# Weight pieces behind the experts' read-back, and Pool's scatter ahead of its gather

## The reference

```python
def _moe(h, router_w, router_bias, w_gate, w_up, w_down):
    x = h.reshape(b * n, d)
    scores = jax.nn.sigmoid(x @ router_w)
    ...  # best group of experts, then the two best experts in it
    gates = jnp.sum(jax.nn.one_hot(idx, N_EXPERTS) * wsel[..., None], axis=1)
    a = jnp.einsum('td,edf->tef', x, w_gate)
    up = jnp.einsum('td,edf->tef', x, w_up)
    mid = jax.nn.silu(a) * up * gates[:, :, None]
    y = jnp.einsum('tef,efd->td', mid, w_down)

def layer(x, l, mod, mixer):
    y, aux = mixer(_rmsnorm(x, norm_mix[l]) * (1.0 + sc1) + sh1)
    x = x + g1 * y
    h = _rmsnorm(x, norm_ffn[l]) * (1.0 + sc2) + sh2
    x = x + g2 * _moe(h, ...)
```

## Time and profile before

| | us |
|---|---|
| median of three runs | 930.47 |
| the three runs | 928.52, 930.5, 930.47 |
| the profiled execution | 928.82 |
| its span, first to last instruction | 927.0 |

### The profile page before, as it was taken

The page is one execution under the profiler, slowest core; times in us unless marked ns, Lnnn a source line. Parts: engine busy times, 40 slices in busy tenths (PEclk is TensorE's granted clock), DMA queues, the critical chain, the costliest instruction groups (busy, mean ns, idle before and its releaser), DMA issues.

```text
span 927.0 us, 11593 instructions
## 1 busy us (share of the span) xinstructions
PE 803.5 (87%) x4091; PEld 447.8 (48%) x4091; DVE 379.2 (41%) x848; ACT 272.2 (29%) x636; POOL 108.1 (12%) x157
## 2 busy tenths in 40 slices
PE   4779999999888996999988599888899978999860
PEld 0236665544443464555536346545554555555430
DVE  3366583265064243332212644664651432322114
ACT  1241212121451042222211536565540332222111
POOL 2300000001000003101013002212200022010120
PEclk9989999999978997899999799999989998999995
DMA  9991222259991347899997966202109388999975
GB/s 275 370 341 50 71 93 95 90 172 345 258 371 53 130 134 250 315 405 410 411 387 262 347 246 246 93 1 93 48 1 346 125 288 312 396 411 410 384 257 208
DMA packets 84561, 220.19 MB, mean 238 GB/s; under 512 B 9636, under 2 KB 19549, under 8 KB 84185
## 3 DMA queue, kind: packets, MB, share of 16 engines
q1 hardware_dynamic: 73570, 197.04, 58.9%
q0 software_dynamic: 9120, 18.75, 5.9%
q10 hardware_dynamic: 1816, 3.68, 1.1%
HBM read 214.77 MB, written 14.89 MB: 248 GB/s over the span
## 4 chain that ended last, share of the span: by engine, by line
PE 63%; DMA 15%; DVE 8%; ACT 4%; SPq 3%; issue 3%; DVEq 1%; POOLq 1%; POOL 0%; ACTq 0%
PE ps L923 57%; PE ps L930 4%; DMA arena<-in_moe_w_up_dram 3%; DMA ring<-in_w_mod_dram 2%; DMA h_rows<-xn 2%; PE ps L1150 2%; DMA ring<-in_moe_w_down_dram 2%; DMA xn<-y_rows 2%; SPq L643 1%; DVEq L1909 1%; DVE negmax L1962 1%; SPq L660 1%; DMA hT<-h_rows,rows_in 1%; SPq L690 1%; ACT hT L1626 1%
## 5 line engine op out<-in xcount | busy, mean ns | idle before, releaser
L923 PE MATMUL ps<-arena 128*64 128x256 f32 (+12 forms) x1164 | 237.6, 449 | 24.8 <-ACT hT L1626 5.9
L923 PEld LDWEIGHTS ps<-arena 128*64 128x64 f32 (+4 forms) x1164 | 128.6, 168 | 115.9 <-issue 71.9
L923 PE MATMUL ps<-ring,hT 128*128 128x512 f32 (+2 forms) x384 | 133.6, 507 | 4.5 <-issue 3.9
L923 PE MATMUL ps<-ring,arena 128*64 128x256 f32 (+1 forms) x784 | 111.3, 431 | 5.5 <-DMA ring<-in_moe_w_down_dram 4.2
L923 PEld LDWEIGHTS ps<-ring,hT 128*128 128x128 f32 x384 | 73.0, 192 | 62.9 <-issue 58.5
L923 PEld LDWEIGHTS ps<-ring,arena 128*64 128x64 f32 x784 | 53.9, 137 | 51.3 <-issue 28.3
L930 PE MATMUL ps<-ident,arena 128*128 128x128 f32 (+2 forms) x332 | 51.0, 293 | 17.2 <-DVE hT L1968 4.6
L1582 ACT ACTIVATE arena<-ps 128x256 f32<-128x256 f32 (+4 forms) x88 | 38.5, 454 | 85.9 <-PE ps L923 82.2
L923 PE MATMUL ps<-hT,ring 128*128 128x384 f32 x192 | 62.1, 486 | 0.0
L2294 DVE TENSOR_TENSOR arena<-arena,ps 128x128 f32<-128x128 f32 x37 | 10.6, 288 | 124.1 <-ACT arena L1688 124.1
L923 PE MATMUL ps<-ring,condT 128*32 128x512 f32 x384 | 52.7, 674 | 8.6 <-DMA ring<-in_w_mod_dram 7.9
(11 more groups left out here) (301 smaller groups left out, 871.7 us busy)
## 6 DMA issues: line engine op xcount, KB each, us to landing
ring<-in_w_mod_dram SPq DMA_DIRECT2D x48, 1024.0 KB, 9.4
ring<-in_moe_w_down_dram SPq DMA_DIRECT2D x22, 1024.0 KB, 16.8
ring<-in_moe_w_gate_dram SPq DMA_DIRECT2D x38, 512.0 KB, 12.9
ring<-in_moe_w_up_dram SPq DMA_DIRECT2D x38, 512.0 KB, 15.5
arena<-in_moe_w_gate_dram SPq DMA_DIRECT2D x36, 512.0 KB, 9.5
arena<-in_moe_w_up_dram SPq DMA_DIRECT2D x36, 512.0 KB, 10.9
arena<-in_moe_w_down_dram SPq DMA_DIRECT2D x15, 1024.0 KB, 13.7
ring<-in_ev_w_in_dram SPq DMA_DIRECT2D x9, 1024.0 KB, 13.3
```

The costliest lines, as they stand in the source:

```text
L923: mm = pe.matmul(out, lhsT, rhs, **kw)
```

## The change

Two places. On SP, `rows_back(0, nb)` is called ahead of the pieces in1.0 and in1.1 instead of behind them. In Pool's overflow loop the pair of waits and the scatter of block b come first, and the pair of waits and the gather of block b + 1 behind it. The waits stay with their DMA.

```diff
@@ SP
                 if i == at["after0"]:
                     nb = send_over(0)
+                if i == at["in1.0"]:
+                    rows_back(0, nb)
                 if i == at["in1.1"] + 1:
-                    rows_back(0, nb)
                     for t in range(NT):
                         sp.wait_ge(y_back[t], 32)
@@ Pool
                 with pool.Fori(1, nb) as b:
                     pool.drain()
+                    pool.wait_ge(over_done[l], b + 1)
+                    pool.wait_ge(y_read[1][l], b + (NE + 1))
+                    pool.tensor_tensor(pool_mark[:, 0:1], pool_mark[:, 0:1], pool_mark[:, 0:1], ALU.mult)
+                    pool.indirect_dma_start(y_rows, bass.IndirectOffsetOnAxis(ap=to_now[0:HALF, :], axis=0), ysb[0:HALF, 0, :], None,
+                                            bounds_check=2 * T - 1, oob_is_err=False).then_inc(over_stored[l], 16)
                     pool.wait_ge(row_ready[l], b + 2)
                     pool.wait_ge(xt_full[1][l], b + (NPAIR + 2))
-                    pool.tensor_tensor(pool_mark[:, 0:1], pool_mark[:, 0:1], pool_mark[:, 0:1], ALU.mult)
+                    pool.tensor_tensor(pool_mark[:, 1:2], pool_mark[:, 1:2], pool_mark[:, 1:2], ALU.mult)
                     pool.indirect_dma_start(xg_over, None, h_rows[l], bass.IndirectOffsetOnAxis(ap=row_now[:, :], axis=0), bounds_check=T - 1, oob_is_err=False).then_inc(
                         over_gathered[l], 16)
-                    pool.wait_ge(over_done[l], b + 1)
-                    pool.wait_ge(y_read[1][l], b + (NE + 1))
-                    pool.tensor_tensor(pool_mark[:, 1:2], pool_mark[:, 1:2], pool_mark[:, 1:2], ALU.mult)
-                    pool.indirect_dma_start(y_rows, bass.IndirectOffsetOnAxis(ap=to_now[0:HALF, :], axis=0), ysb[0:HALF, 0, :], None,
-                                            bounds_check=2 * T - 1, oob_is_err=False).then_inc(over_stored[l], 16)
```

## The result

The changed kernel takes 940.35 us (median of six runs, 938.91 to 946.6), the kernel before beside it 930.49 us. The ratio is 1.0139, with a 95% interval from 1.0103 to 1.0175: 10 to 16 us slower. The forecast was 934.9 us with a range up to 937.4: the direction was right, the size less than half.

A forecast was written before the change was run, and what follows sets the result against it. Bound by hand-overs between Pool, TensorE and the DMA queues at the ends of both layers' experts. Layer 0 +0.45 and layer 1 +3.95 make +4.4 us, set on the 930.47 us median: 934.9 us, range 931.0 to 937.4.

The forecast's parts named there:

- part 2: Pool's overflow loop, scatter first, then gather: +1.05 us in layer 0, +2.9 and +1.05 us in layer 1.
- ACT's reads start 1.05 us late, SP's don't: Layer 0's read-back: ACT waits for the loop's last gather; +1.05 us charged whole, bounds 0 and 1.6; same in layer 1.
- the ring: Sign in layer 0: the latent projection should show no wait on it; waiting for the in1 pieces would refute the forecast.
- My bound of zero: ACT's late read-back in layer 0: lowest cost 0, since SP's head start uses the same bandwidth and nothing is lost.
- The gather of block 1 sooner: Layer 0: without 1.7 MB of in1 pieces beside it, the gather lands 0.6 us sooner; bounds 0 and 1.54.
- The scatter without the gather ahead of it: Layer 0's last scatter: losing the gather ahead is worth nothing, 498.25 at the earliest against 498.35.
- The in1 pieces hidden: Layer 0: the moved pieces land at 517.6, before the latent projection at 521.48; 3 to 4 us of slack, no cost.
- Rival 3: Layer 0: in1 pieces at half rate land at 522, TensorE stands some 2 us; 936.9 us, chance 0.10.
- The late gather of block 2: Layer 1: starts at 896.32 instead of 891.96, lands in 4.05 us; down product +2.9 us, bounds +1.0 and +3.7.
- Rival 1: Both layers: the late gathers are hidden, layer 0 -0.6 and layer 1 +1.0 us; 930.9 us, chance 0.16.
- Rival 2: Layer 0's traffic is the bound: 1.54 us from the in1 pieces, 1.8 from Pool's loads; 927.2 us, chance 0.08.

The follow-up runs named there:

- e5: The kernel before with only ACT's three reads held back by four tiny activations (0.48 us) in both layers; 935.48 us, ratio 1.0053.
- e6: The kernel before with SP's three reads held until ACT has issued its own; 936.11 us, ratio 1.0067.
- e3: The changed kernel with ACT's wait for the gathers moved behind its three reads in both layers; 932.53 us, ratio 1.0028 against the kernel before.
- e11: The kernel before with the in1 pieces behind the read-back and Pool's nine MLA loads held until the read-back has landed; 929.86 us, ratio 1.0017.
- e2: The kernel before with only the in1 pieces moved behind the read-back, the loop still gather first; 928.94 us, ratio 0.9993.
- e1: The kernel before with only the loop order changed to scatter first, the in1 pieces still ahead of the read-back; 939.68 us, ratio 1.0114.
- e8: The kernel before with Pool's nine small MLA loads held until the read-back has landed; 929.78 us, ratio 0.9974.
- e10: The changed kernel with ACT's wait for the gathers behind its reads in layer 0 only; 936.65 us, +6.3 us against the kernel before.
- e7: The changed kernel with 52 instead of 28 filling products on TensorE in layer 0's read-back; 942.96 us, ratio 1.0120 against the kernel before.

## Why the prediction was wrong

**The step that failed** is in part 2: "ACT's reads start 1.05 us late, SP's don't ... so I charge all of it", and the same for layer 1. The place was right, and the delay nearly so: 0.95 us in both layers. The price was wrong. I charged the length of the delay, and held 0 and 1.6 us for its bounds. It costs 2.6 us in layer 1, and in layer 0 4.25 us at the latent products, of which about 1 us goes with the in1 pieces. The signs that the prediction named for this all came: ACT's reads 1 us behind SP's, a wait for the gather of block 2, none for the ring. None of them was the landing of ACT's first tile.

The forecast assumed that from the moment ACT's reads are issued, each queue gets half. The traces show that with a head start of 0.95 us SP's first two tiles go out alone. In layer 1 SP's tiles landed about 3.7, 5.0 and 7.5 us after its start, ACT's first at 7.65; before, with both together, SP's landed at 4.7, 7.3 and 9.8, ACT's first at 5.1. e5 gives the slope with nothing else changed, e6 shows it with the roles changed, and e3 takes it away.

The bytes weren't lost: in layer 1 the last of the six tiles is there 10.1 us after the start in both kernels. The order changed, and each join needs both halves of the first tile. My bound of zero ("SP's head start uses the same bandwidth and nothing is lost") reasoned from the total, where the chain hangs on the first tile.

The Trainium skill ("DMA: Bandwidth & Descriptors", Queues, rings and completion order) says that a DMA engine takes turns between its queues, packet by packet. I let that rule stand for an even division from ACT's start on. The traces agree with the turns once both queues move: 5 to 6 us after the start (920.24 to 921.24) SP's moved 0.20 MB and ACT's 0.22. They don't show them from ACT's issue on. This is what the queues moved in the first 4 us (packets, MB, share of 16 engines; q1 is SP's, q10 ACT's), in the kernel before from 905.61 to 909.61:

```profile
q1 hardware_dynamic: 126, 0.50, 46.9%
q10 hardware_dynamic: 107, 0.44, 28.0%
```

and in the changed one from 915.24 to 919.24, where q10 has no row, though ACT had issued its first tile after 0.95 us:

```profile
q1 hardware_dynamic: 252, 0.97, 73.2%
```

ACT's queue began when SP's had moved about 1.1 MB, two tiles. In e5, issued 0.52 us late, it began after 0.6 MB, about one tile, and in e6 SP's began after 1.3 MB of ACT's. That fits tiles that go out in the order of their issue, whichever queue they are on. No run tests this by itself, and why the later queue starts so late isn't settled.

**What I left out** is TensorE's clock. I had not weighed this row: the latent products of the kernel before take 7.22 us for 16, though those behind them need 11.41 us for 32. In the profiled execution the changed kernel pays 1.24 us and 1.7 us in layer 0, and 1.1 us on the last down product in layer 1 (3.02 us instead of 1.94). The first two come back later. Nor do they follow from the delay alone: in e6 TensorE stood 11.68 us ahead of the transposes and these products took 7.27 and 5.76 us, nearly as before; in e11 it stood 6.26 us, less than before, and they took 8.77 and 7.46. The third goes with the long wait for the late gather (see e3).

**Point by point.**
- *The gather of block 1 sooner.* Forecast -0.6 us. It took 7.43 us instead of 7.84 and TensorE waited 1.04 us instead of 1.54: 0.4 to 0.5 us, right. It didn't help the total: e2 is -0.7 us with 2.4 us to each side.
- *The scatter without the gather ahead of it.* Forecast worth nothing. VectorE ended 0.11 us sooner and the scatter started 0.11 us sooner: right, with the 0.53 us between mark and issue that an idle Pool needs.
- *The in1 pieces hidden.* No wait on them is in any trace, right as far as TensorE is concerned. Rival 3 looked at TensorE, which doesn't wait for them. What they cost is seen at ACT's tiles, and it is a small part: the latent products start 20.5 us after SP's reads in the kernel before, 23.9 us in e1, 24.9 us here.
- *The late gather of block 2.* Forecast: it lands in 4.05 us, the down product starts 2.9 us late. It landed in 3.1 us (3.2 before), and the down product was 2.1 us late, with 1.1 us more for the clock. e3 and e2 differ by 3.2 us. The sum was right, its parts not. The Trainium skill (same page and section) says that a completion increment lands only after every earlier write of the same DMA engine. This trace agrees with it: the down weights landed at 905.2, the scatter at 905.5, the gather at 905.7, in the order of their issue. (The order of issue is not always that of landing: in the kernel before a gather issued 0.7 us after the weights landed at 889.15, they at 889.91. The rule is for each DMA engine, which these times of whole DMAs don't separate.) The three DMAs of the changed kernel, with the time from issue to landing at the end:

```profile
arena<-in_moe_w_down_dram SPq DMA_DIRECT2D x1, 1024.0 KB, 4.9
y_rows<-arena,ck POOLq DMA_INDIRECT x1, 4.2
hT<-h_rows,row_now POOLq DMA_INDIRECT x1, 3.1
```

- *Rival 1* (hidden) falls with the result, and e3, whose lower end is just above zero, speaks against it for the late gather by itself. *Rival 2* (layer 0's traffic) had the 1.8 us of the loads right at the read-back, and e8 shows why they are worth a third of that; of its 1.54 us for the in1 pieces 0.5 came.

**The range** ended at 937.4 since no bound held a price larger than the delay itself, and none a lower clock.

**What stays open**: why the later queue starts so late; how much of the lower clock in layer 0 arrives at the end; and 2.2 us at about 860 us, in one execution, which no edit explains.

## What to carry to other kernels

When two queues bring the halves of one thing, start them together. Here a late start of one cost two to six times its length at the first tile, in layer 1 with the last tile no later than before. So before an instruction is moved behind another, list every wait, on every engine, that counts it, also where its result is used by nobody (here a gather for a block that doesn't exist), and put such waits behind the DMAs they don't guard. And where a delay makes TensorE idle, look at the granted clock of what comes next and price it apart.

## What the runs showed of the hardware

- Two queues with three 512 KB reads each, from SP and ACT: with starts 0.00, 0.52 and 0.95 us apart, the later one's first tile came 5.1, 6.5 and 7.65 us after the earlier one's start in layer 1; with SP 1.67 us behind, 8.26 us. Other kernels with 0.92 to 0.95 us gave 7.6 (e10), 8.3 (e1) and 8.5 us (e7). In layer 0, beside other transfers, the times were 5.2, 7.0 and 8.5 us (10.8 in e7), and 10.45 us with SP behind.
- The later queue moved nothing in the first 4 us when it was issued 0.95 us late; once it moved, the two moved 0.20 and 0.22 MB in the same microsecond.
- Pool's gather with no row within bounds took 2.2 us to land in layer 0 of the kernel before, and 2.17 and 2.13 us behind a scatter in the changed kernel.
- An indirect DMA behind its mark instruction on Pool: the issue starts 0.53 us after the mark when Pool had been idle (L862) and 0.15 us when it had just issued another (L867).
- The granted clock fell in an idle stretch of 4.7 us between transposes and latent products although TensorE had been busy for 22.7 us and on the transposes before it (e7: 1.16 us for the transposes, as at the full clock, then 8.27 us for the latent products, against 7.22 in the kernel before).
- The last down product of layer 1 took 2.83 to 3.68 us in the five traces with a wait of 2.7 to 2.9 us ahead of its transposes, and 1.94 us in the other eight.
